# Weight sums of a Strassen-Winograd tail by accumulating DMAs, squared relu on ACT, and the weights' low parts on VectorE in the up stages

## The reference

```
x = x + gate1 * (concat([pool_out, attn_out]) @ w_out)
h2 = rmsnorm(x, g_mlp) * (1 + scale2) + shift2
x = x + gate2 * (square(relu(h2 @ w_up)) @ w_down)
y = rmsnorm(x, g_final)
```

## Time and profile before

| | |
|---|---|
| median of three runs | 1592.62 us |
| the profiled execution | 1598.2 us, span of its instructions 1596.4 us |
| busy share of TensorE, VectorE, ACT, GpSimd | 87%, 76%, 39%, 49% |
| mean granted clock of TensorE | 0.925 |
| tail | from 571.6 us to the end |

### The profile page before, as it was taken

How to read it: one execution, slowest core, us unless ns; L and a number is a source line. 1 busy time by engine, 2 the same in 40 slices (tenths; PEclk the granted TensorE clock), 3 DMA queues, 4 the chain that set the end, 5 groups by cost and what they waited for, 6 DMA issues and landing times. The chain is left out here.

```text
span 1596.4 us, 29541 instructions
## 1 busy us (share of the span) xinstructions
PE 1390.5 (87%) x11700; PEld 1249.5 (78%) x11700; DVE 1214.1 (76%) x1765; ACT 617.2 (39%) x1259; POOL 779.9 (49%) x558
## 2 busy tenths in 40 slices
PE   5999999999899989785988979969879788897986
PEld 4999866666677678785977979969879788897886
DVE  4836565656677548889988689898698986899885
ACT  5512655554133343454432335323334223352234
POOL 0032132224122165346875677676478755888440
PEclk8999999999799999897998989989989899898888
DMA  9511343247477640200200200201002001011003
GB/s 353 202 49 60 104 150 115 78 146 218 194 259 252 211 165 1 80 1 33 98 9 28 80 1 28 80 16 65 27 27 80 1 28 54 1 53 54 1 1 112
DMA packets 65907, 140.17 MB, mean 88 GB/s; under 512 B 13511, under 2 KB 20627, under 8 KB 61539
## 3 DMA queue, kind: packets, MB, share of 16 engines
q1 hardware_dynamic: 58785, 100.45, 18.6%
q0 software_dynamic: 5760, 37.75, 6.7%
q10 hardware_dynamic: 1226, 0.08, 0.1%
HBM read 122.24 MB, written 13.79 MB: 85 GB/s over the span
## 5 line engine op out<-in xcount | busy, mean ns | idle before, releaser
L1316 PE MATMUL psa<-x_hi,w_hi 128*128 128x272 f32 x2016 | 619.2, 307 | 145.6 <-DVE xT L2379 79.3
L1316 PE MATMUL psa<-x_hi,w_lo 128*128 128x272 f32 x2016 | 605.1, 300 | 0.0
L1316 PE MATMUL psa<-x_lo,w_hi 128*128 128x272 f32 x2016 | 604.6, 300 | 0.0
L1316 PEld LDWEIGHTS psa<-x_hi,w_hi 128*128 128x128 f32 x2016 | 406.0, 201 | 167.3 <-issue 114.5
L1316 PEld LDWEIGHTS psa<-x_lo,w_hi 128*128 128x128 f32 x2016 | 405.5, 201 | 0.2
L1316 PEld LDWEIGHTS psa<-x_hi,w_lo 128*128 128x128 f32 x2016 | 404.9, 201 | 0.0
L777 POOL TENSOR_TENSOR w_lo<-quarter,w_hi 128x512 fp32r<-128x512 f32 x172 | 258.8, 1504 | 292.3 <-ACT w_hi L1748 292.0
L777 POOL TENSOR_TENSOR w_lo<-s_sum,w_hi 128x512 fp32r<-128x512 f32 x72 | 116.2, 1615 | 46.8 <-ACT w_hi L1748 46.8
L2379 DVE SCALAR_TENSOR_TENSOR xT<-psa,modT,xT 128x272 f32<-128x272 f32 (+1 forms) x280 | 117.0, 471 | 0.0
L1771 ACT ACTIVATE x_hi<-t_sum 128x544 fp32r<-128x544 f32 x72 | 47.6, 661 | 176.5 <-DVE t_sum L2349 94.4
L1771 ACT ACTIVATE x_hi<-t_tmp 128x544 fp32r<-128x544 f32 x71 | 47.2, 664 | 175.5 <-PE psa L1316 141.4
(11 more groups left out here) (326 smaller groups left out, 2664.1 us busy)
## 6 DMA issues: line engine op xcount, KB each, us to landing
wmod<-in_w_mod SPq DMA_DIRECT2D x8, 2048.0 KB, 8.4
quarter<-in_w_up SPq DMA_DIRECT2D x16, 1024.0 KB, 5.3
quarter<-in_w_down SPq DMA_DIRECT2D x16, 1024.0 KB, 5.2
...
quarter<-in_w_out SPq DMA_DIRECT2D x4, 1024.0 KB, 6.6
xstage<-in_x_prompt SPq DMA_DIRECT2D x3, 1024.0 KB, 10.6
```

The lines of the kernel that those rows point to most:

```text
L1316: mm = pe.matmul(tail_bank(p, i)[:, 0:HB], a[:, i * P:i * P + P], x[:, HB * p:HB * p + HB], start=(m in OPENS and k == 0 and q == 0), stop ...
```

## The change

Weights. Sums of quarters are no longer made on GpSimd, except in stage 0. The sums are built in the weight buffers themselves, of which there are six now: SP loads one quarter, and GpSimd's queue then issues DMAs that add further quarters to the buffer (`add_weights`, `accum_op=ALU.add`). `W_BUFFERS` says which buffer a product reads, `ADDED` which quarters it holds by then. M1's A11 becomes M7's sum by one more; M5 holds two quarters; M6 three, and with a fourth it is M3's. Up to then differences are needed, so the algorithm is turned: the output rows of half 1 are computed negated, and the signs of gates (`modT` from row 4 of each gate on), activation sums and evictions follow. Each add waits for the load or add before it, and for the low part of the buffer's last use.

Low parts. In up stages `w_low` is done by VectorE, behind `x_low`; in the other stages by GpSimd as before. `wait_low` counts the two kinds apart.

Squared relu. ACT does it (`squared`), as a relu and a square of each 128x544 tile, for M4 with the relu already in `first_kept`.

Samples. `residual` adds the sample columns of each product to an accumulator (`acc_s`), ungated; `keep_samples` applies the gates and adds the accumulator to xT, once for each half of the rows in stage 0 and once for each in stage 8.

```diff
-W_SUMMED = [('M5', 'M3', 'M7') if o is LATE else ('M6', 'M7', 'M5', 'M3') for o in ORDERS]
+W_SUMMED = [('M5', 'M3', 'M7')] + [()] * (STAGES - 1)
+FIRST = {0: ('M1', 'M4'), 2: ('M6', 'M7'), 4: (), 6: (), 8: ()}
...
+W_BUFFERS = [{'M5': 5, 'M3': 4, 'M6': 5, 'M1': 2, 'M7': 2, 'M4': 1, 'M2': 3}]
+W_BUFFERS += [{'M2': 0, 'M1': 2, 'M6': 5 - w % 2, 'M7': 2, 'M4': 1, 'M5': 3, 'M3': 5 - w % 2} for w in range(1, STAGES - 1)]
+W_BUFFERS += [{'M5': 0, 'M3': 5, 'M1': 2, 'M6': 0, 'M7': 2, 'M4': 1, 'M2': 3}]
+ADDED = {'M2': ('A12',), 'M1': ('A11',), 'M6': ('A21', 'A22', 'A11'), 'M7': ('A11', 'A21'), 'M4': ('A22',), 'M5': ('A21', 'A22'),
+         'M3': ('A21', 'A22', 'A11', 'A12')}
+PARTS = [[max((ADDED[m] for m in ADDED if W_BUFFERS[w][m] == b), key=len, default=()) for b in range(6)] for w in range(STAGES)]
+PARTS[0] = [('A21',), ('A22',), ('A11',), ('A12',), (), ()]
...
-    quarters = [at(f"quarter{k}", [P, 4, 512], F32, R0 + o) for k, o in enumerate((92160, 75776, 58368, 33792, 83968))]
-    s2_sum = at("s2_sum", [P, 4, 512], F32, R0 + 17408)
...
+    def wait_low(eng, j):
+        if place(j)[0] % 2:
+            eng.wait_ge(sem("w_low_dve"), DVE_LOWS[j])
+        else:
+            eng.wait_ge(sem("w_low"), POOL_LOWS[j])
+    def wait_weights(eng, w, m):
+        b = W_BUFFERS[w][m]
+        if w == 0 or len(ADDED[m]) == 1:
+            eng.wait_ge(sem(f"quarter_in{b}"), BEFORE[f"quarter_in{b}"] + 16 * (loads_before(w, b) + 1))
+        else:
+            eng.wait_ge(sem(f"added_in{b}"), BEFORE[f"added_in{b}"] + 16 * (adds_before(w, b) + len(ADDED[m]) - 1))
...
+        def load_weights(w, b):
+            sp.dma_start(quarters[b][:, :, :], w_part(w, PARTS[w][b][0])).then_inc(sem(f"quarter_in{b}"), 16)
...
-        sp.wait_ge(sem("x_low"), 2)
-        load_quarter(1, 'A12')
...
+        sp.wait_ge(sem("w_low"), 8)
+        load_weights(1, 4)
+        sp.wait_ge(sem("w_low"), 16)
+        load_weights(2, 5)
+        sp.wait_ge(sem("w_low"), 20)
+        load_weights(1, 2)
+        load_weights(1, 0)
+        sp.wait_ge(sem("w_low"), 24)
+        load_weights(1, 1)
+        sp.wait_ge(sem("w_low"), 28)
+        load_weights(1, 3)
...
+            for pos, b in enumerate((0, None, None, 2, 1, 3, 5 - (w + 1) % 2)):
+                if b is None or w == STAGES - 1 and pos == 6:
+                    continue
+                wait_low(sp, STEPS * (w - 1) + 4 * pos + 3)
+                load_weights(w + (pos == 6), b)
...
+            elif m == 'M3':
+                g.wait_ge(sem("quarter_in2"), BEFORE["quarter_in2"] + 16)
+                g.wait_ge(sem("quarter_in3"), BEFORE["quarter_in3"] + 16)
+                g.wait_ge(sem("at_mm"), 1)
+                g.wait_ge(sem("x_low"), 2)
+                chain(g.tensor_tensor(s2, s2, a11, ALU.add))
+                s = g.tensor_tensor(s4, a12, s2, ALU.add)
...
+        def add_weights(w, b, n):
+            if n == 1:
+                g.wait_ge(sem(f"quarter_in{b}"), BEFORE[f"quarter_in{b}"] + 16 * (loads_before(w, b) + 1))
+            else:
+                g.wait_ge(sem(f"added_in{b}"), BEFORE[f"added_in{b}"] + 16 * (adds_before(w, b) + n - 1))
+            g.dma_start(quarters[b][:, :, :], w_part(w, PARTS[w][b][n]), accum_op=ALU.add).then_inc(sem(f"added_in{b}"), 16)
...
-            w_low(j)
+            if place(j)[0] % 2 == 0:
+                w_low(j)
+            w, r = divmod(j, STEPS)
+            if w < STAGES - 1 and r == 12:
+                add_weights(w + 1, 4 + w % 2, 1)
+            if w < STAGES - 1 and r == 20:
+                add_weights(w + 1, 4 + w % 2, 2)
+            if 0 < w < STAGES - 1:
+                if r == 7:
+                    wait_low(g, j)
+                    add_weights(w, 2, 1)
+                if r == 9:
+                    add_weights(w, 3, 1)
+                if r == 11:
+                    wait_low(g, j)
+                    add_weights(w, 5 - w % 2, 3)
+            if w == STAGES - 2 and r == 9:
+                add_weights(w + 1, 0, 1)
+            if w == STAGES - 2 and r == 25:
+                add_weights(w + 1, 5, 3)
+            if w == STAGES - 1 and r == 3:
+                wait_low(g, j)
+                add_weights(w, 0, 2)
+            if w == STAGES - 1 and r == 11:
+                wait_low(g, j)
+                add_weights(w, 2, 1)
...
-            pe.wait_ge(sem("w_low"), j + 1)
+            wait_low(pe, j)
...
-                wait_quarter(act, w, {'M2': 'A12', 'M1': 'A11', 'M4': 'A22'}[m])
+                wait_weights(act, w, m)
...
-                act.activation(g_all[:, c, c0:c0 + HB], out[:, 0:HB], ACT.Copy).then_inc(sem("unit_kept"), 1)
+                act.activation(g_all[:, c, c0:c0 + HB], out[:, 0:HB], ACT.Relu if m == 'M4' else ACT.Copy,
+                               scale=-1.0 if m in ('M7', 'M4') else 1.0).then_inc(sem("unit_kept"), 1)
+        def squared(phase, pair):
+            m = ORDERS[phase // 7][phase % 7]
+            tiles = []
+            for i in (2 * pair, 2 * pair + 1):
+                out, c, c0, u = unit_tile(phase, 4 + i)
+                tiles.append(g_all[:, c, c0:c0 + HT])
+            act.wait_ge(sem("unit_kept"), u + 1)
+            if m != 'M4':
+                act.activation(tiles[0], tiles[0], ACT.Relu)
+                chain(act.activation(tiles[1], tiles[1], ACT.Relu))
+            act.activation(tiles[0], tiles[0], ACT.Square).then_inc(sem("g_done"), 1)
+            act.activation(tiles[1], tiles[1], ACT.Square).then_inc(sem("g_done"), 1)
...
             if j % 4 == 3 and w % 2 and m in ('M2', 'M6', 'M7', 'M4'):
                 first_kept(phase)
+            if j % 4 < 2 and j >= 8:
+                phase = (j - 8) // 4
+                w, m = phase // 7, ORDERS[phase // 7][phase % 7]
+                if w % 2 and m in ('M1', 'M4', 'M5', 'M3'):
+                    squared(phase, j % 4)
...
             if m == 'M5':
-                s = tt(x_piece(j), b12, b11, ALU.subtract)
+                s = tt(x_piece(j), b11, b12, ALU.subtract)
             elif m == 'M6':
-                chain(tt(t2, b22, b12, ALU.subtract))
-                s = tt(t2, t2, b11, ALU.add)
+                chain(tt(t2, b12, b22, ALU.subtract))
+                s = tt(t2, t2, b11, ALU.subtract)
...
+            if place(j)[0] % 2:
+                v.wait_ge(sem("w_high"), j + 1)
+                tt(w_lo[j % 4][:, :], w_piece(j), w_hi[j % 4][:, :].bitcast(F32), ALU.subtract).then_inc(sem("w_low_dve"), 1)
...
-                new = xT[:, c, TP:T].rearrange("p (b s) -> p b s", b=NB)
-                gates = modT[:, gate, 1:9].unsqueeze(2).to_broadcast([P, NB, NS])
-                chain(tt(tmp_s[:, :, :], out[:, N:HB].rearrange("p (b s) -> p b s", b=NB), gates, ALU.mult))
-                tt(new, new, tmp_s[:, :, :], ALU.add)
+                if ORDERS[w][phase % 7] in FIRST[w]:
+                    v.tensor_copy(acc_s[:, c, :], out[:, N:HB])
+                else:
+                    tt(acc_s[:, c, :], out[:, N:HB], acc_s[:, c, :], ALU.add)
...
-            v.scalar_tensor_tensor(out=cols, in0=cols, scalar=0.0, in1=cols, op0=ALU.max, op1=ALU.mult).then_inc(sem("g_done"), 1)
+            cols = g_all[:, c, c0:c0 + HB]
+            if c < 4:
+                tt(cols, out[:, 0:HB], cols, ALU.add).then_inc(sem("unit_kept"), 1)
+            else:
+                tt(cols, cols, out[:, 0:HB], ALU.subtract).then_inc(sem("unit_kept"), 1)
+        def keep_samples(phase, row_half, gate):
+            v.wait_ge(sem("unit_kept"), 8 * phase + 8)
+            rows = slice(4 * row_half, 4 * row_half + 4)
+            acc, x = acc_s[:, rows, :].rearrange("p k (b s) -> p k b s", b=NB), xT[:, rows, TP:T].rearrange("p k (b s) -> p k b s", b=NB)
+            gates = modT[:, gate + 4 * row_half:gate + 4 * row_half + 4, 1:9].unsqueeze(3).to_broadcast([P, 4, NB, NS])
+            chain(tt(acc, acc, gates, ALU.mult))
+            tt(x, x, acc, ALU.add).then_inc(sem("samples_kept"), 1)
 
         def kept(phase):
...
+            if w in (0, STAGES - 1) and m == ('M4', 'M6')[w > 0]:
+                keep_samples(phase, w == 0, M_G2 if w else M_G1)
+            if w in (0, STAGES - 1) and m == ('M2', 'M7')[w > 0]:
+                keep_samples(phase, w > 0, M_G2 if w else M_G1)
...
+        for gate in (M_G1 + 4, M_G2 + 4):
+            chain(v.tensor_scalar(modT[:, gate:gate + 4, 0:9], modT[:, gate:gate + 4, 0:9], -1.0, 0.0, ALU.mult, ALU.add))
...
-                if phase in (7 * STAGES - 9, 7 * STAGES - 8):
-                    for i in range(4):
-                        activated(phase, i)
-            if j % 4 < 2 and j >= 8:
-                phase = (j - 8) // 4
-                w, m = phase // 7, ORDERS[phase // 7][phase % 7]
-                if phase not in (7 * STAGES - 9, 7 * STAGES - 8) and w % 2 and m in ('M1', 'M4', 'M5', 'M3'):
-                    activated(phase, 2 * (j % 4))
-                    activated(phase, 2 * (j % 4) + 1)
```

(14 more changed lines are left out.)

114 lines of the change are left out of this document (34 added, 80 removed), and 1 row of the table SHARED.

## The result

The changed kernel takes **1433.2 us** (median of four runs, 1428.5 to 1435.8). The kernel before took 1595.6 us beside it on the same chip (four runs, the three shown among them). The ratio is 0.898 (95% interval 0.893 to 0.903), so 162 us less. The forecast was 1465: the direction was right and so was the mechanism of the long waits. The time is 32 us lower than said, and 7 us under the low end of the range.

The account below looks back on a forecast made before the run. VectorE's work before M6, lengthened by GpSimd's sums, was taken to bound the kernel. Gains 57 (down), 51 (up), 9, 3 and 12 (stages 1, 0, 8) sum to 132: 1460.6, said as 1465 allowing for uncovered waits; range 1440 to 1565.

Parts of the forecast that it names:

- The bound and its cause: Before M6, GpSimd operations each cost VectorE about 1.0 us; without weight sums, a down stage's 10.3 us stall becomes 2.7.
- rival 4: The long waits are not GpSimd's doing and only sample evictions gain: about 1585 us; chance 0.06.
- Adds hidden: Accumulating DMAs, five a stage, land after 15 us with about 20 available for M7's, and cost no time.
- rival 1: Adds land late: from 20 us each us costs 1 us in each of eight stages; at 28 us, 1530; chance 0.13.
- rival 3: Slower than before: M7's add lands after more than 36 us; at 45 us, 1665 us; chance 0.09.
- VectorE in up stages: With low parts added and squarings gone, VectorE has 11.2 us of work in M1's 12.0; 0.5 us of stall left.
- rival 2: In up stages VectorE's operations stay above 0.9 us, M1 and M6 windows take 15 us or more: 1525; chance 0.12.
- Squared relu on ACT: In up stages, 28 more ACT passes, 18.5 us, cost nothing, and the 2.7 us stall before M3 goes.
- Half clock: TensorE's slow clock costs about 6 us in a down stage; 2 left there, 1.5 in an up stage.
- the two sums behind it: Stage times with all leftovers above the 84 us floor: down stage 92 us, up stage 88.5 us.
- The samples' part: In four phases of a down stage, sample evictions and their waits take 10 us before and 2 after.
- The low end: Lower edge of the forecast range, 1440 us: no allowance for newly exposed waits, and the adds hidden.

Follow-up runs that it names:

- e3: Changed kernel with GpSimd's weight sums in place of the accumulating DMAs, with the signs and weight buffers of the kernel before: 1493.1 us.
- e7: Changed kernel plus twelve GpSimd sums of SBUF constants, output unused, around M1 in each of stages 3, 5 and 7: 1460.8 us.
- e8: Changed kernel plus twelve GpSimd memsets, which write and read nothing, around M1 in each of stages 3, 5 and 7: 1435.0 us.
- e5: Changed kernel with each product's sample columns gated and added to xT again, three operations a unit: 1494.3 us.
- e9: Changed kernel with M7's add (A21 onto A11) issued four steps later, in stages 1 to 7: 1487.1 us.
- e4: Changed kernel with the low parts of the weights on GpSimd in all stages: 1437.3 us.
- e6: Changed kernel with the squared relu back on VectorE, M4's relu included: 1433.8 us.

## Why the prediction was right in kind and 32 us short

- **The bound and its cause: right.** The long waits were GpSimd's doing; rival 4 is refuted by e3, where GpSimd's sums alone keep the 10.3 us in down stages, and by e7, where 12 reading operations bring 5.9 us of wait into the M1 window of a kernel that had none. The price, 1.0 us of VectorE for each GpSimd operation (1.1 in the rows above, 1.82 - 0.72), gave 2.7 us before M6 and 2.5 were measured. The Trainium skill ("SBUF — State Buffer", Who interferes with whom) has the same split that e7 and e8 show, between GpSimd instructions that read SBUF and those that only write it. It also says that a VectorE instruction with at most one SBUF input, outside the two-port modes, is free of it: the trace agrees, L2436 (one PSUM, one SBUF input) took 206 to 218 ns in all 60 cases of the changed kernel, 32 of which overlapped a GpSimd sum or low part, while L2438 of e5 (two SBUF inputs, same size) took 224 to 226 ns in the 47 cases without such an overlap and up to 1264 ns in the 29 with one. By an estimate from the exclusive lock that the same section of the Trainium skill ("SBUF — State Buffer", Who interferes with whom) has, 1.27 us an operation in place of 1.0, 3.8 us would have been left; the measurement stays with 1.0.
- **Adds hidden: right, and rivals 1 and 3 fell.** They landed after 8.8 us in the median (8.3 to 18.1), where I took 15, and the M7 add had some 19 to spend; e9 shows that on the far side the price is steeper than the 1 us per us that rival 1 was given. Engine time: 24.9% of 1426.7 us less 6.7% of 1596.4 is 248 us for 41 adds, 6.1 us each, against 6.2 assumed. An issue held GpSimd 1.28 us, not 0.93, without effect.
- **VectorE in up stages: right, rival 2 fell.** x_lo has a mean of 0.72 us in stage 3, and TensorE doesn't wait. The account of why was too narrow: by e3 and e4 either of two edits would have done most of it, since GpSimd's sums leave the M1 window by themselves once its low parts are gone.
- **Squared relu on ACT: right at no cost.** The wait before M3 that it was to remove goes with the other parts as well (e6).
- **The step that failed is what was left standing beside the one long wait, in "Half clock" and in the two sums behind it.** I let 2 us of half clock stay in a down stage and 1.5 in an up stage, with 2 more in a down stage for samples, 0.5 for the wait before M6 and 1.5 for ACT's evictions in an up stage, 0.5 for M2's start, 1 and 0.5 unlisted, and put 4.4 on the whole. Nothing of this but up to 1.9 us of busy time was there: down stages took 86.9, 88.4 and 86.8 us for 92 said, up stages 84.2, 84.2 and 85.2 for 88.5. For the clock, ACT's evictions and the unlisted ones no row was given. The size before was a remainder as well (26.6 - 10.3 - 10 = 6 us). As clock it was near, 5.3 us in stage 4; but the window row had 8.9 us of busy time above 84, and the waits besides the long one were 7.3, not 10. So the forecast had no term for the short waits that hide in busy time. e5 shows the link: twelve short waits in a down stage come with 7.5 us of busy time, at a clock of 0.93, and both go together.
- **The samples' part was mis-sized with it**: 8 us a down stage said, 13.5 measured in stage 4 (15 in stages 2 and 6), of which 6.0 are waits. Its price was its waits and the busy time that hangs on them.
- **Smaller terms.** Stage 1: 13.9 for 9 (its standing time alone gained 9.4). Stage 0: 2.1 for 3. Stage 8: 17.0 for 12, although it stands only 4.3 us less; the busy time that went, 12.7 us, is mostly clock, since TensorE was busy 29.8 us at half clock there and is 9.8.
- **The low end** was built with the leftovers in it. With the wait of 2.7 us before M6 and nothing else above 84 us, three down stages come to 260 and three up stages to 252 us: 73 + 65 in place of 57 + 51, and the whole to 1592.6 - 162 = 1431 us. That is the case the range had to hold, and 1433 was measured. (That the two agree so well is luck in part: stages 0, 1 and 8 gained 9 us more than said, the down and up stages 4 less than this sum has, and the kernel before ran 3 us slower.)

In numbers, the spans of the traces fell by 169.7 us where the sum less its allowance said 127.6: 14.0 more in down stages, 12.4 in up stages, 4.9 in stage 1, 5.0 in stage 8, 0.9 less in stage 0, the allowance of 4.4, and 2.3 ahead of the tail that belong to no edit. This is the pair of traces; between the medians it is 162.
